# Attention weights fetched straight into place, with stores, seeds and scaling reordered

## The reference

```python
def _diff_attention(p, lam_params, subln, rel_bias, layer):
    q, k, v = jnp.split(p, 3, axis=-1)
    ...
        logits = jnp.einsum('bqhmd,bkhmd->bmhqk', qb, k).astype(jnp.float32) + bias
        probs = jax.nn.softmax(logits, axis=-1)
        w = (probs[:, 0] - lam * probs[:, 1]).astype(v.dtype)
        return jnp.einsum('bhqk,bkhe->bqhe', w, v)
    ...
    o = _rms_norm(o, subln) * (1.0 - lam_init)

def reference(...):
    ...
        y = jnp.concatenate([mixed, recalled], axis=-1) @ w_o[layer]
        x = _layer_norm(ALPHA * x + y, ln_gain[layer, 0], ln_bias[layer, 0])
        f = _conv_ffn(x, ffn_w_up[layer], ffn_conv[layer], ffn_w_down[layer])
        x = _layer_norm(ALPHA * x + f, ln_gain[layer, 1], ln_bias[layer, 1])
```

## Time and profile before

| | us |
|---|---|
| Median of 3 runs (1243.75 to 1246.12) | 1246.05 |
| Profiled execution | 1246.42 |
| Its span, first to last instruction | 1244.6 |
| TensorE busy | 1229.6 |
| VectorE busy | 1036.6 |
| ScalarE busy | 724.6 |

### The profile page before, as it was taken

How to read it: one execution, slowest core, us unless ns; L and a number is a source line. 1 busy time by engine, 2 the same in 40 slices (tenths; PEclk the granted TensorE clock), 3 DMA queues, 4 the chain that set the end, 5 groups by cost and what they waited for, 6 DMA issues and landing times.

```text
span 1244.6 us, 19585 instructions
## 1 busy us (share of the span) xinstructions
PE 1229.6 (99%) x7290; PEld 1076.8 (87%) x7290; DVE 1036.6 (83%) x1613; ACT 724.6 (58%) x1178; POOL 20.0 (2%) x29
## 2 busy tenths in 40 slices
PE   9999999999999999999999999999999999999997
PEld 8978888888999998888888888888888978888886
DVE  6886888888879888988888978988888786988887
ACT  6665755555776546655554546655554674755552
POOL 0000000000000000000000000000000001000000
PEclk9999999999999999999999999999999999999999
DMA  9865576655454345666555775665665664666651
GB/s 330 276 210 186 186 245 189 197 179 180 161 182 132 119 139 168 224 198 201 188 186 170 249 248 168 223 199 194 194 185 171 213 212 135 217 208 202 194 192 54
DMA packets 79993, 239.75 MB, mean 193 GB/s; under 512 B 8694, under 2 KB 24694, under 8 KB 78876
## 3 DMA queue, kind: packets, MB, share of 16 engines
q1 hardware_dynamic: 79900, 238.51, 58.5%
HBM read 232.18 MB, written 6.30 MB: 192 GB/s over the span
## 4 chain that ended last, share of the span: by engine, by line
PE 88%; DVE 4%; DMA 3%; ACT 3%; SPq 1%; issue 1%; DVEq 0%; ACTq 0%
PE pair L842 28%; PE acc L936 21%; PE pair L845 14%; PE pair L874 3%; PE pair L875 3%; PE pair L876 3%; PE pair L1103 2%; PE acc L917 2%; PE acc L915 2%; PE acc L916 2%; PE acc L842 1%; DMA raw<-in_stream 1%; ACT ex L1298 1%; DVE w_lo L1364 1%; DMA swap_scratch<-prob 1%
## 5 line engine op out<-in xcount | busy, mean ns | idle before, releaser
L1364 DVE TENSOR_TENSOR w_lo<-raw,w_hi 128x1024 fp32r<-128x1024 f32 x400 | 482.3, 1220 | 92.0 <-ACT w_hi L1121 90.7
L1121 ACT ACTIVATE w_hi<-raw 128x1024 fp32r<-128x1024 f32 x400 | 420.3, 1057 | 226.3 <-PE pair L845 69.5
L842 PE MATMUL pair<-xT,w_hi 128*128 128x512 f32 x1520 | 477.8, 396 | 0.2 <-DVE w_lo L1364 0.2
L845 PEld LDWEIGHTS pair<-xT,w_lo 128*128 128x128 f32 x1520 | 285.5, 188 | 67.2
L845 PE MATMUL pair<-xT,w_lo 128*128 128x256 f32 x1520 | 298.6, 278 | 0.0
L842 PEld LDWEIGHTS pair<-xT,w_hi 128*128 128x128 f32 x1520 | 233.7, 189 | 3.5 <-DVE w_lo L1364 0.4
L1168 ACT ACTIVATE hid<-pair 128x512 f32<-128x512 f32 x88 | 52.6, 597 | 125.0 <-PE pair L845 125.0
L1405 DVE TENSOR_TENSOR hid<-pair,hid 128x512 f32<-128x512 f32 x88 | 60.7, 690 | 47.8 <-ACT hid L1168 47.4
L874 PE MATMUL pair<-xT,w_hi 128*128 128x256 f32 x336 | 97.4, 290 | 0.0
L875 PE MATMUL pair<-xT,w_hi 128*128 128x256 f32 x336 | 95.0, 283 | 0.0
L876 PE MATMUL pair<-xT,w_lo 128*128 128x256 f32 x336 | 94.9, 283 | 0.0
(11 more groups left out here) (229 smaller groups left out, 1653.5 us busy)
## 6 DMA issues: line engine op xcount, KB each, us to landing
raw<-in_stream SPq DMA_DIRECT2D x400, 512.0 KB, 4.7
gains<-in_ln SPq DMA_DIRECT2D x8, 1024.0 KB, 8.7
swap_scratch<-ex SPq DMA_DIRECT2D x24, 128.0 KB, 2.4
bias<-bias_scratch SPq DMA_DIRECT2D x2, 1152.0 KB, 10.9
raw<-in_stream SPq DMA_DIRECT2D x8, 256.0 KB, 6.3
swap_scratch<-prob SPq DMA_DIRECT2D x32, 64.0 KB, 4.0
a_sq<-swap_scratch SPq DMA_DIRECT2D x8, 256.0 KB, 2.8
xprobT<-swap_scratch SPq DMA_DIRECT2D x3, 512.0 KB, 3.9
```

What stands on the lines that cost most here:

```text
L842: pe.matmul(bank, w_hi[:, slot, kk * P:(kk + 1) * P], xT[:, kk].rearrange("p a s -> p (a s)"), start=(kk == 0), stop=(kk == KT - 1), skip_ ...
L845: last = pe.matmul(bank[:, 0:SEQ], w_lo[:, slot, kk * P:(kk + 1) * P], xT[:, kk, 0, :], start=False, stop=(kk == KT - 1), skip_group_check ...
L1121: nc.scalar.activation(w_hi[:, u % SPLIT, :], raw[:, u % RAW, :], ACT.Copy).then_inc(hi_ready, 1)
L1364: v.tensor_tensor(w_lo[:, u % SPLIT, :], raw[:, u % RAW, :], w_hi[:, u % SPLIT, :].bitcast(F32), ALU.subtract).then_inc(lo_ready, 1)
```

## The change

In the schedule of the attention layers the fetch of head 0 moves behind the transpose and the stores of head 1. The four copies (`spread`) disappear. The second seed moves from the row behind the probabilities of head 4 to a place ahead of the exponentials of head 5. The probabilities of head 5 move behind the scaling of the first pair of heads. In layer 2 the probabilities, stores and fetch of the second memory pair move from row 3 to row 6.

A fetch of heads 0 to 3 becomes four DMAs, one for each block of 32 queries. Each has 512 pieces of 128 bytes and lands in `probT` itself, in final order. The semaphore of landed fetches counts 64 for such a head and 16 for a memory pair (`landed_count`). SP no longer waits for copies, and TensorE's products of heads 0 to 3 wait for the landing.

```diff
@@ -125,18 +125,18 @@
-                  8: [it("prob", 0), it("swap", 0), it("fetch", 0)],
-                  9: [it("prob", 1), it("swap", 1), it("fetch", 1), it("log", 2), it("log", 3)],
+                  8: [it("prob", 0), it("swap", 0)],
+                  9: [it("prob", 1), it("swap", 1), it("fetch", 0), it("fetch", 1), it("log", 2), it("log", 3)],
                   10: [it("exp", 2)], 11: [it("exp", 3), it("prob", 2), it("swap", 2), it("fetch", 2), it("xpv", 0), it("xpv", 1)],
-                  12: [it("prob", 3), it("swap", 3), it("fetch", 3), it("spread", 0)],
-                  13: [it("spread", 1), it("log", 4), it("log", 5)],
-                  14: [it("pv", 0), it("pv", 1), it("ms", 0), it("exp", 4)], 15: [it("tok", 0), it("exp", 5), it("prob", 4)],
-                  16: [it("spread", 2), it("prob", 5)], 17: [it("spread", 3), it("scale", 0)],
+                  12: [it("prob", 3), it("swap", 3), it("fetch", 3)],
+                  13: [it("log", 4), it("log", 5)],
+                  14: [it("pv", 0), it("pv", 1), it("ms", 0), it("exp", 4)],
+                  15: [it("tok", 0), ("seed", 2 * layer, 1), it("exp", 5), it("prob", 4)],
+                  17: [it("scale", 0), it("prob", 5)],
                   18: [it("turnw", 4), it("pv", 2), it("pv", 3), it("turnw", 5)],
...
             at[14].append(("seed", 2 * layer, 0))
-            at[16].append(("seed", 2 * layer, 1))
@@ -147,7 +147,7 @@
-                  3: [it("xprob", 1), it("xswap", 1), it("xfetch", 1)], 13: [it("xpv", 0), it("xpv", 1)]}
+                  6: [it("xprob", 1), it("xswap", 1), it("xfetch", 1)], 13: [it("xpv", 0), it("xpv", 1)]}
@@ -275,12 +275,14 @@
-    swap_count, swap_ord, turned_ord, seen = {}, {}, {}, {}
+    swap_count, swap_ord, turned_ord, landed_count, seen, landed = {}, {}, {}, {}, {}, {}
...
+            landed[n % 2] = landed.get(n % 2, 0) + (16 if item[0] == "xswap" else 64)
+            landed_count[n] = landed[n % 2]
@@ -614,7 +616,7 @@
             if name == "prob":
-                place = a_sq[:, 1 + h % 2]
+                return probT[:, h].rearrange("p t k (a j) -> p a (t k) j", a=4)
@@ -718,13 +720,17 @@
-                        sp.wait_ge(swap_landed[n % 2], 16 * (swap_count[n] - 1))
-                    if name == "fetch" and item[2] >= 2:
-                        sp.wait_ge(probT_ready, HEADS * (item[1] // 3) + item[2] - 1)
+                        sp.wait_ge(swap_landed[n % 2], landed_count[n] - (64 if name == "fetch" else 16))
...
                     sp.wait_ge(swap_stored[n % 2], 64 * swap_count[n])
-                    sp.dma_start(swap_target(n), swap_scratch[n].rearrange("a b i e -> (b i) a e")).then_inc(swap_landed[n % 2], 16)
+                    blocks = swap_scratch[n].rearrange("a b i e -> (b i) a e")
+                    if name == "fetch":
+                        for a in range(4):
+                            sp.dma_start(swap_target(n)[:, a], blocks[:, a].rearrange("p (c j) -> p c j", j=32)).then_inc(
+                                swap_landed[n % 2], 16)
+                    else:
+                        sp.dma_start(swap_target(n), blocks).then_inc(swap_landed[n % 2], 16)
@@ -1048,7 +1054,11 @@
                     layer, h = item[1:]
-                    pe.wait_ge(probT_ready, HEADS * (layer // 3) + h + 1)
+                    n = weights_of(item)
+                    if n in turned_ord:
+                        pe.wait_ge(probT_ready, turned_ord[n])
+                    else:
+                        pe.wait_ge(swap_landed[n % 2], landed_count[n])
@@ -1305,11 +1315,6 @@
-                elif name == "spread":
-                    n = prob_ord["", item[1], item[2]]
-                    act.wait_ge(swap_landed[n % 2], 16 * swap_count[n])
-                    nc.scalar.activation(probT[:, item[2]].rearrange("p t k (a j) -> p (t k) a j", a=4),
-                                         swap_target(n).rearrange("p a (c j) -> p c a j", j=32), ACT.Copy).then_inc(probT_ready, 1)
```

More of the change, by code:

```diff
@@ L591, in side_read @@
             if name == "turnw":
-                return probT_ready, HEADS * (item[1] // 3) + item[2] + 1
+                return probT_ready, turned_ord[prob_ord["", item[1], item[2]]]
             return {"bias_rows": rows_ready, "xpv": xmix_ready}[name], u + 1
@@ L1035, in _ @@
                     if n in swap_count:
-                        pe.wait_ge(swap_landed[n % 2], 16 * swap_count[n])
+                        pe.wait_ge(swap_landed[n % 2], landed_count[n])
                         weights = swap_target(n).rearrange("p a (i t k j) -> p i k t a j", i=2, t=2, k=2)
```

## The result

| | us |
|---|---|
| Before, median of 6 runs (1243.75 to 1246.29) | 1245.93 |
| Changed, median of 6 runs (1247.90 to 1252.94) | 1250.68 |
| Ratio, with its 95% interval | 1.0048 (1.0038 to 1.0057) |
| Changed, the profiled execution; its span | 1252.34; 1250.2 |

The change is slower by 4.75 us, where a gain of 0.6 was forecast. TensorE's work is what it was (1229.6 us in the earlier trace rows); the span is 5.6 us longer. First the page of the changed kernel, part 1.

A forecast was written before the change was run, and what follows sets the result against it. TensorE was busy 1229.6 of 1244.6 us, with a serial chain through SP's queue just under it. Gains of 0.1, 0.1 and 0.4 us summed to -0.6, hence 1245.5 us, range 1242 to 1252.

The forecast's parts named there:

- f: SP's queue time for one head's fetch as four DMAs, until the next issue: taken as 2.1 us, bounds 1.7 to 3.4.
- the forecast's own sum: Gains of 0.1 us in each attention layer and 0.4 in the convolution layer: -0.6 us, giving 1245.5 us.
- The chain: Stores, landing, fetches, unit 28's load, rounding, eviction, head 5's transposes in series; these start at 100.1 us in layer 0.
- Rival 2: Slower: the small pieces, not the issues, set the pace; up to 1255.9 us at f = 3.4; chance 0.27.
- rival 3: TensorE stands ahead of head 5's transposes, the clock falls again, up to 1.7 us: 1247.2; chance 0.38 together with the forecast.
- Copies: Eight copies leave ScalarE, 0.52 us each; TensorE's 2.0 us wait for a copied weight tile was a target.
- seeds: Second seed of the output sums ahead of head 5's exponentials; targets 2.1 us of TensorE's waiting.
- convolution layer: Second pair's probabilities move behind the gating product; TensorE's wait of 0.4 us goes.
- The 1.9 us on the scaled heads: TensorE's wait in two pieces, targeted by fewer copies and later head 5 probabilities; win bounded by 1.04 us in layer 3.

The follow-up runs named there:

- experiment 4: Kernel before with only the change's moves, each fetch as four DMAs of 128 pieces of 512 bytes, still copied by ScalarE: 1247.63 us, ratio 1.0021.
- Experiment 1: Changed kernel, with the four issues of head 3's fetch put behind the weight load that followed them on SP's queue: 1246.04 us, ratio 1.0006.
- experiment 2: Kernel before with stores, seed, probabilities and convolution layer's pair moved, but one DMA of 512-byte rows per head and the copies kept: 1246.13 us, ratio 1.0011.

## Why the prediction was wrong, point by point

- **The step that failed is the price of the fetches, f.** The forecast took 0.43 + 3 x 0.55 = 2.1 us from a load's issue behind a single fetch; measured is 2.60. That lies within the bounds given for f, 1.7 to 3.4; the value chosen inside them was too low. By the forecast's own sum, 4f per layer, that is 4 x 0.5 = 2.0 us more in each layer: 1245.5 + 4.0 = 1249.5, slower, of the measured 1250.68. The row that was used shows a load's issue behind one fetch of longer pieces; experiment 4 shows that an issue grows with the kind of pieces in its DMA. The traces also show that the sum comes near the measured time partly by luck: at the transposes the late load cost 0.5 us in layer 0, since the first fetch left earlier than assumed, and 2.0 in layer 3, 2.5 together and not 4.0. The clock made most of the rest.
- **The chain was right.** It gave the load of unit 28 at 85.37 + 4f = 95.8 with the measured f; it left at 94.88, since the first fetch left at 71.33 where 72.67 was assumed; the waits between the fetches were 0.4 us longer than assumed. From the load to the rounding 4.68 us (4.64 assumed), then the eviction and the transposes, as written. In layer 3, 1013.36 + 4f = 1023.8, and 1027.28 less the 3.70 us by which the kernel was already late is 1023.6. Experiment 1 moved that one load and the wait went; in experiment 4 shorter issues did the same.
- **The rivals.** Rival 2 had the time: 1250.7 at f = 2.75, slower from f = 2.5 on. That it had the time is luck in part, as its mechanism was not the one found: the pieces' data did not set the pace. Its sign was a fetch of over 4 us to landing; the changed kernel's fetches landed 2.2 to 2.7 us after each issue, and the issues took 0.64 us where 0.8 and more were its sign. During the fetch at 94 to 95 us the engines were half idle (DMA queues: packets, MB, share of 16 engines):

```profile
q1 hardware_dynamic: 650, 0.08, 51.3%
```

  That is 0.513 x 16 / 650 = 12.6 ns for a piece of 128 bytes. Over the whole trace of the changed kernel a packet of 128 bytes takes 12.8 ns in the mean, one of 512 bytes 27. A quarter of the bytes costs nearly half of the time, so small pieces are dearer by the byte, but that was not the limit. The Trainium skill says that transfers under 512 B are not at line rate (DMA: Bandwidth & Descriptors, Specifications); these packets agree. Its other rule bears on the limit: by the Trainium skill, Perfetto Trace Analysis, What "DMA-bound" means, an issuing queue solid with DMA slices is bound by the making of descriptors. The 2.55 us rows of SP's queue are solid in this sense; what an issue's time consists of, no row here shows.
- **The clock (rival 3)** was right in kind and too small: 0 to 1.7 us was given, 3.4 us were lost behind layer 0's hole in the profiled execution. Priced as lost TensorE time behind the hole, it is the second part of the loss. It explains the long executions of the moves alone (experiment 2); those at full clock won nothing either.
- **Copies, seeds, convolution layer:** the targeted waits went as said (2.0, 2.1, 0.4). The 1.9 us on the scaled heads, counted among the targets, did not go: head 4's transposes came earlier (95.08 instead of 97.94 in layer 0), but TensorE came earlier still and waited 3.9 us there instead of 1.9.

## What to carry to other kernels

When a DMA is split, count the issues and the pieces of each against the queue they stand in, and look at what is queued behind: here a weight load that nobody changed was what became late, and putting it first, ahead of the issues and of the wait in front of them, took the ratio from 1.0048 to 1.0006. A hole that one removes is worth only the way to the next late thing, and here a TensorE that arrived early and then stood lost clock as well as time; fill the new hole with work that is already there before removing more.

## What was unexpected of the hardware

The issue of a DMA on SP's queue took 2.55 / 4 = 0.64 us in a row with 512 pieces of 128 bytes, and 1.76 / 4 = 0.44 us with 128 pieces of 512 bytes, at equal bytes. A single fetch of 512 pieces took 0.38 us, but the load behind it 0.51, where behind 128 pieces it took 0.43 (experiment 4), so in these rows part of the price falls on the next instruction. Behind the changed kernel's pieces the load's issue took 0.62. And the same program took very different times from one execution to the next: 1247.9 to 1258.2 us over the changed kernel's 17 executions, at mean clocks from 0.998 to 0.994. Not all of that is the clock, as at 0.994 alone they lie from 1252.9 to 1258.2. By contrast, the kernel before, with shorter holes, stayed within 1243.5 and 1247.9.
